# Two-block transformer on one core: the second head of each attention pair is normalised by GpSimd

## The chip, the cores and the metric

One core of a Trainium2 chip runs the whole program. The time is device microseconds of one launch, and the number to forecast is the median over several runs. In the texts "DVE" is VectorE, "ACT" ScalarE, "PE" TensorE, "POOL" GpSimd, "SP" SyncE.

## The reference

The input is x, 256 tokens by 1024 features, float32. A first block of two layers (feed-forward, mixer, cross attention to a memory, feed-forward) is followed by a second block of two layers (mixer of three parts, layer norm, feed-forward, layer norm). Three places hold the attention that the change touches:

```
# mixer of the first block's second layer (latent attention): 16 heads, 256 tokens, keys in the same or an earlier chunk of 64
sc = einsum('bhqd,bhkd->bhqk', q, k) * scale;  sc = where(chunk_mask, sc, -inf)
p = softmax(sc);  o = einsum('bhqk,bhkd->bhqd', p, v)
...
# second block, both layers (sparse attention): 8 heads of width 64
o_slc = selected attention, o_win = window attention      # both causal softmax attention at 256 tokens
o = gate[0] * o_cmp + gate[1] * o_slc + gate[2] * o_win
```

With 256 tokens every block of keys is selected and the window covers all, so the two sparse branches are 16 causal attention heads, each with its own gate.

## The kernel before

The kernel is written without a scheduler: each engine has its own program, and all of them walk the same list of pieces in the same order. The list of a stage comes from a hand-made string (WEAVE, one letter for each piece of a chain), so an engine's instructions stand in the order of the string, and semaphores alone connect the engines. A stage is named m0, m1 (mixers of the first block), c0, c1 (cross attention), f0 to f5 (feed-forward), b0, b1 (mixers of the second block). Weights come by DMA from SP into a ring of 6 buffers (ring), ACT rounds each buffer (w_hi) and DVE subtracts for the rest (w_lo), and PE multiplies with both.

The class Pairs (from L1184) is the attention of m1 and of b0 and b1. A piece ("A", (j, step)) treats pair j, that is two heads p = 0 and 1; there are 8 pairs in m1 and 8 in each of b0 and b1, 24 in all. Scores of a head lie in PSUM as 384 columns: 256 for the second half of the queries, 128 for the first half.

- Step 0: PE makes scores, DVE takes the row maxima (L175), ACT makes exponentials and their sums from PSUM into the head's SBUF buffer (L147).
- Step 1: DVE makes reciprocals of the four sums (L178), in b0 and b1 multiplies them by the gate (L158, 128x4), and scales each head's buffer in place: one TENSOR_SCALAR of 128x256 and one of 128x128 (L164). The second of the two signals "scaled" for its head. PE waits for "scaled" of head 0, transposes its three 128x128 blocks (L138), then does the same for head 1. ACT copies the transposed blocks out (L184, 128x384).
- Step 2: PE multiplies by the values, and the result is evicted.

In m1 the string puts step 1 of four pairs in a row, twice: once right behind the first scores, once near the stage's end, before the output product. In b0 and b1 the pairs are woven among the chains of the recurrent mixer (letters r and s), whose pieces also use POOL: piece "ru" masks three 128x1024 tiles (L158), and piece "nc" zeroes two small tiles (L197) and has DVE shift and add its input tiles (L185, L158 128x120) before PE's compression product.

POOL's part in m1 is only the squares for the next norm at the stage's end. In each stage POOL walks its pieces in the order of the string as well, and a wait holds up everything behind it on its queue.

```
# the step 1 of DVE, the lines that matter
        for p in range(2):
            x = A.s(j, p)
            e.ts(x[:, 0:256], x[:, 0:256], r[:, 2 * p + 1:2 * p + 2], None, MUL)
            e.ts(x[:, 256:384], x[:, 256:384], r[:, 2 * p:2 * p + 1], None, MUL).then_inc(*e.up("scaled", (A.name, j, p)))
```

Of the kernel before, what the change touches and what calls it, by code (L numbers as in the profile page):

```python
# [13 lines left out]
MUL, ADD, SUB, MIN, MAX = ALU.mult, ALU.add, ALU.subtract, ALU.min, ALU.max  # L14
# [665 lines left out]
def pool_x(e, K, s, j):  # L680

    n = AFTER[s]
    if j < 8 and n in NORMED:
        e.wait_ge(*K.x_at(s, j))
        x = K.x[:, j, :]
        if j == 0:
            e.then(e.tt(K.squares, x, x, MUL))
        else:
            e.then(e.tt(K.square, x, x, MUL), *(("squares", n) if j == 7 else ()))
            if j < 7:  # L690
                e.then(e.tt(K.squares, K.squares, K.square, ADD))
# [148 lines left out]
def pool_ln(e, K, s, what, i):  # L840
    half, dev, sq, M, squares = ln_area(K)
    x = K.x
    if what == "x" and 0 < i < 4:
        for k in (0, 1) if i == 1 else (i,):
            e.wait_ge(*K.at("evicted", (s, "x", last_of(s, k))))
        e.then(e.tt(half, x[:, 0, :] if i == 1 else half, x[:, i, :], ADD), *(("ln_half", s) if i == 3 else ()))
    elif what == "ld" and 0 < i < 7 and s[0] == "f":
        for k in (0, 1) if i == 1 else (i,):
            e.wait_ge(*centred(K, s, k))
            e.wait_ge(*K.at("ln_squares", (s, k)))  # L850
        e.tt(dev, x[:, 0, :] if i == 1 else dev, x[:, i, :], ADD)
        e.then(e.tt(sq, squares[:, 0, :] if i == 1 else sq, squares[:, i, :], ADD), *(("ln_added", s) if i == 6 else ()))
    elif what == "lm":
        e.wait_ge(*K.at("ln_means", s))
        for k in range(8):
            e.tt(x[:, k, :], x[:, k, :], M, SUB).then_inc(*e.up("ln_shifted", (s, k)))
# [327 lines left out]
class Pairs:  # L1184
# [20 lines left out]
    def stat(self, j, n, p=None):  # L1205
        c = self.stats[self.lane(j)][:, 4 * n:4 * n + 4]
        return c if p is None else c[:, 2 * p:2 * p + 2]

    def chains(self, what, names):
        out = {}  # L1210
        for name, js in zip(names, self.lanes):
            c = [(what, (js[0], 0)), (what, (js[0], 1))]
            for a, b in zip(js, js[1:]):
                c += [(what, (b, 0)), (what, (a, 2)), (what, (b, 1))]
            out[name] = c + [(what, (js[-1], 2))]
        return out
# [54 lines left out]
def dve_pairs(e, K, A, j, step):  # L1271
    if step == 0:
        for p in range(2):
            e.wait_ge(*K.at("scores", (A.name, j, p)))
            b, m = K.psum((A.name, j, "s", p)), A.stat(j, 0, p)
            e.red(m[:, 1:2], b[:, 0:256], MAX, negate=True)
            ins = e.red(m[:, 0:1], b[:, 256:384], MAX, negate=True)
            if not A.factor:
                ins.then_inc(*e.up("maxima", (A.name, j, p)))
        if A.factor:  # L1280
            e.then(ins)
            e.wait_ge(*K.at("factor", A.name))
            m = A.stat(j, 0).rearrange("p (a t) -> p a t", a=2)
            e.tt(m, m, A.factor(j), MUL).then_inc(*e.up("maxima", (A.name, j, None)))
    elif step == 1:
        for p in range(2):
            e.wait_ge(*K.at("evicted", (A.name, j, "s", p)))
        r = A.stat(j, 2)
        e.then(e.rec(r, A.stat(j, 1)))
        if A.gate:  # L1290
            r2 = r.rearrange("p (a q) -> p a q", a=2)
            e.then(e.tt(r2, r2, A.gate(j), MUL))
        for p in range(2):
            x = A.s(j, p)
            e.ts(x[:, 0:256], x[:, 0:256], r[:, 2 * p + 1:2 * p + 2], None, MUL)
            e.ts(x[:, 256:384], x[:, 256:384], r[:, 2 * p:2 * p + 1], None, MUL).then_inc(*e.up("scaled", (A.name, j, p)))


def in_lanes(what, units, lanes, steps=3):
# [10 lines left out]
def evenly(chains):  # L1310

    at = sorted(((n + 0.5) / len(c), k) for k, c in chains.items() for n in range(len(c)))
    return "".join(k for _, k in at)


def woven(stage, chains):

    for mark, piece in MARKS.items():
        chains[mark] = [(piece, i) for i in range(WEAVE.get(stage, "").count(mark))]
    its = {k: iter(c) for k, c in chains.items()}  # L1320
    return [next(its[k]) for k in WEAVE.get(stage) or evenly(chains)]
# [909 lines left out]


def pool_mla(e, K, T, what, i):
    if what == "x":
        pool_x(e, K, T.stage, i)

# [353 lines left out]

def pool_block(e, K, T, what, i):
    e.wait_ge(K.S.sem("loaded_c" + T.area), 16)
    s = T.stage
    if what in LN + ("x",):
        pool_ln(e, K, s, what, i)
    elif what[0] == "r":
        pool_delta(e, K, T, what, i)
    elif what[0] == "g":
        pool_gla(e, K, T, what, i)
    elif what == "nc" and i == 0:  # L2600
        e.wait_ge(*K.at("gated", (s, "g")))
        e.set(T.kc, 0.0)
        e.set(T.hid[0:64], 0.0).then_inc(*e.up("zeroed", (s, "hid")))
# [397 lines left out]
def pool_delta(e, K, T, what, i):  # L3001
    s, V = T.stage, T.block_of(what, i)
    m4 = T.c32.unsqueeze(2).broadcast_to([128, 4, 256])
    if what == "rp" and i == 0:
        e.wait_ge(*K.at("split_x", (s, 7)))
        e.set(T.PR[:, :, 0:1], 0.0).then_inc(*e.up("zeroed", (s, "PR")))
    elif what == "ri" and i == (0, 0):
        e.wait_ge(*K.at("turned", (s, "rtm", 3)))
        for n in [(s, "rp", 4), (s, "gp", 2), (s, "gl")] + [((s, "np", n), t) for n in range(3) for t in range(2)]:
            e.wait_ge(*K.at("summed", n))  # L3010
        e.set(T.Pt, 0.0)
        e.set(T.Q, 0.0)
        e.set(T.St[:, :, 0, :], 0.0).then_inc(*e.up("zeroed", (s, "r")))
    elif what == "ru" and i[1] == 1:
        tb = i[0]
        e.wait_ge(*K.at("evicted", (s, "rtm", 1)))
        e.wait_ge(*K.at("summed", (s, "ri", tb, (6, "r7"))))
        e.tt(V.Bm, bc(T.Btm[:, tb, :], 4), m4, MUL).then_inc(*e.up("masked", (s, tb, "B")))
        e.wait_ge(*K.at("evicted", (s, "rtm", 3)))
        e.tt(V.Vm, bc(T.Vtm[:, tb, :], 4), m4, MUL)  # L3020
        e.wait_ge(*K.at("evicted", (s, "ru", tb, 1)))
        e.tt(V.TUm, bc(V.AV, 4), m4, MUL).then_inc(*e.up("masked", (s, tb, "U")))
# [182 lines left out]
def pool_gla(e, K, T, what, i):  # L3205
    s = T.stage
    if what == "gd":
        for j in range(2):
            e.wait_ge(*K.at("evicted", (s, "gp", j)))
        e.tt(T.gE[2], T.gq, T.gk, MUL).then_inc(*e.up("pairs", s))  # L3210
    elif what == "gx" and i == 0:
        B = T.gB[:, :, 0:128]
        e.wait_ge(*K.at("scanned", (s, "g")))
        e.tt(T.XK[1][:, :, 0:128], B[:, :, 127:128].broadcast_to([128, 2, 128]), B, SUB).then_inc(*e.up("differences", (s, "x")))
    elif what == "ge" and i[1] == 0:
        n = i[0]
        h = HALVES[n]
        B, E = (a.rearrange("p k (c i) -> p k c i", i=2 * h) for a in (T.gB, T.gE[n % 3]))
        if n == 2:
            e.wait_ge(*K.at("summed", (s, "gd")))  # L3220
        elif n > 2:
            e.wait_ge(*K.at("scaled", (s, n - 3)))
        e.wait_ge(*K.at("scanned", (s, "g")))
        e.tt(E, B, B[:, :, :, h - 1:h].broadcast_to([128, 2, 128 // h, 2 * h]), SUB).then_inc(*e.up("differences", (s, n)))
# [219 lines left out]
ACTE = {"ffn": act_ffn, "mixer0": act_mixer0, "cross": act_cross, "mla": act_mla, "block": act_block}  # L3444
DVE = {"ffn": dve_ffn, "mixer0": dve_mixer0, "cross": dve_cross, "mla": dve_mla, "block": dve_block}
POOL = {"ffn": pool_ffn, "mixer0": pool_mixer0, "cross": pool_cross, "mla": pool_mla, "block": pool_block}

def stages(K):
# [149 lines left out]
```

## Time and profile before

| what | value |
|---|---|
| runs | 2096.41, 2089.3, 2094.63 us; median 2094.63 |
| profiled execution, its own time | 2091.17 us |
| its span | 2089.1 us |
| PE busy | 1971.4 us (94% of the span) |
| DVE busy | 1504.5 us (72%) |
| ACT busy | 1115.3 us (53%) |
| POOL busy | 400.7 us (19%), 357 instructions |
| chain that ended last | PE 82%, DVE 10%, ACT 5% |

The page gives busy time per engine over the whole span; which engine sets the pace differs from stage to stage, so the chain of waits and the timelines of the stages are read as well. The attention steps of m1 lie between about 855 and 887 us, those of b0 between 1300 and 1364 us, those of b1 between 1769 and 1851 us.

### The profile page before, as it was taken

How to read it: one execution, taken by the hardware profiler on the slowest of the kernel's cores; microseconds unless marked ns; L12 is line 12 of the kernel's file. 1: busy time of each engine (PE TensorE's matmuls, PEld its weight loads, DVE VectorE, ACT ScalarE, POOL GpSimd, SP SyncE). 2: the span in 40 equal slices, each digit the busy share in tenths (PEclk: the TensorE clock that was granted, in tenths of full speed). 3: DMA queues.
4: the chain of work that ended last, by engine and by line, in shares of the span. 5: the costliest groups of instructions: out<-in, count | busy, mean ns of one | idle time of the engine just before them, and what ended most of it. 6: DMA issues, size and time to landing. Idle time of an engine off the chain costs nothing.

```text
span 2089.1 us, 32759 instructions
## 1 busy us (share of the span) xinstructions
PE 1971.4 (94%) x12454; PEld 1720.6 (82%) x12454; DVE 1504.5 (72%) x2640; ACT 1115.3 (53%) x2048; POOL 400.7 (19%) x357
## 2 busy tenths in 40 slices
PE   7999999999999999899999997899998988899997
PEld 6888888888888887698888887688887877688886
DVE  6976876787678778768776696667756697567765
ACT  5654566565455556745554533556545444357554
POOL 3521002222112210023210101102213011101213
PEclk9999999999999999999999999999998999899999
DMA  7556443455565555135555321236553421225652
GB/s 252 197 175 194 159 131 122 132 190 178 186 191 188 174 190 165 55 121 194 187 179 176 125 88 41 87 111 219 189 176 110 139 76 41 77 94 169 191 182 82
DMA packets 88716, 309.81 MB, mean 148 GB/s; under 512 B 9840, under 2 KB 11632, under 8 KB 88176
## 3 DMA queue, kind: packets, MB, share of 16 engines
q1 hardware_dynamic: 88272, 305.03, 44.5%
q10 hardware_dynamic: 288, 2.69, 0.4%
q8 instruction: 99, 1.62, 0.3%
q14 instruction: 57, 0.47, 0.1%
HBM read 306.63 MB, written 1.05 MB: 147 GB/s over the span
## 4 chain that ended last, share of the span: by engine, by line
PE 82%; DVE 10%; ACT 5%; issue 2%; POOL 1%; DMA 1%; SPq 0%; DVEq 0%; ACTq 0%; POOLq 0%
PE ps L133 80%; DVE scratch L158 3%; ACT scratch L147 3%; PE ps L138 2%; POOL rows L158 1%; DVE w_lo L158 1%; DVE scratch L164 1%; DVE scratch L185 1%; DVE stats L175 1%; DVE x L158 1%; ACT w_hi L147 1%; DMA ring<-in_w 1%; DVE scratch L170 0%; ACT scratch L184 0%; ACT L152 0%
## 5 line engine op out<-in xcount | busy, mean ns | idle before, releaser
L133 PE MATMUL ps<-h,w_hi 128*128 128x512 f32 (+1 forms) x2912 | 903.0, 371 | 27.6 <-DVE w_lo L158 15.9
L158 DVE TENSOR_TENSOR w_lo<-ring,w_hi 128x1024 fp32r<-128x1024 f32 (+3 forms) x573 | 695.8, 1225 | 301.0 <-ACT w_hi L147 297.3
L147 ACT ACTIVATE w_hi<-ring 128x1024 fp32r<-128x1024 f32 (+3 forms) x573 | 583.5, 1029 | 419.1 <-PE ps L133 414.4
L133 PE MATMUL ps<-h,w_lo 128*128 128x256 f32 x2512 | 709.7, 283 | 0.0
L133 PEld LDWEIGHTS ps<-h,w_hi 128*128 128x128 f32 x2912 | 529.3, 192 | 132.0 <-issue 20.0
L133 PEld LDWEIGHTS ps<-h,w_lo 128*128 128x128 f32 x2512 | 481.2, 192 | 0.0
L133 PE MATMUL ps<-f,w_hi 128*128 128x512 f32 (+1 forms) x1444 | 419.1, 357 | 0.1
L133 PE MATMUL ps<-f,w_lo 128*128 128x256 f32 x1184 | 332.5, 281 | 0.0
L158 POOL TENSOR_TENSOR f<-f_work,f 128x256 fp32r<-128x256 f32 x132 | 188.0, 1425 | 583.3 <-ACT f L147 583.2
L133 PEld LDWEIGHTS ps<-f,w_hi 128*128 128x128 f32 x1444 | 254.9, 189 | 43.2 <-DVE scratch L158 0.3
L133 PEld LDWEIGHTS ps<-f,w_lo 128*128 128x128 f32 x1184 | 224.5, 190 | 0.1
L133 PE MATMUL ps<-scratch 64*128 64x128 f32 (+10 forms) x1696 | 196.4, 317 | 22.2 <-DVE scratch L158 10.2
L133 PEld LDWEIGHTS ps<-scratch 64*128 64x128 f32 (+4 forms) x1696 | 160.0, 180 | 54.0 <-issue 21.0
L184 ACT ACTIVATE scratch<-ps 128x512 f32<-128x512 f32 (+9 forms) x196 | 90.8, 487 | 195.6 <-PE ps L133 157.2
L158 POOL TENSOR_TENSOR rows<-x 128x256 f32<-128x256 f32 x64 | 54.1, 846 | 478.8 <-DVE x L158 470.0
L158 DVE TENSOR_TENSOR f_work<-f_work,ps 128x256 f32<-128x256 f32 x306 | 126.4, 414 | 3.6 <-ACT f_work L184 3.5
L158 DVE TENSOR_TENSOR f_work<-f_work 128x256 f32<-128x256 f32 x264 | 114.2, 433 | 8.6
L133 PE MATMUL ps<-w_hi,h 128*128 128x512 f32 (+2 forms) x384 | 113.9, 374 | 0.7 <-DVE w_lo L158 0.7
L184 ACT ACTIVATE f_work<-ps 128x256 f32<-128x256 f32 x306 | 110.9, 365 | 1.3 <-PE ps L133 1.3
L138 PE MATMUL ps<-consts,scratch 128*128 128x128 f32 (+3 forms) x428 | 68.5, 296 | 32.5 <-DVE scratch L164 12.9
L147 ACT ACTIVATE scratch<-ps,stats 128x256 f32<-128x256 f32 (+2 forms) x143 | 68.8, 500 | 48.0 <-PE ps L133 27.1
L158 DVE TENSOR_TENSOR scratch<-scratch 128x512 f32<-128x512 f32 (+7 forms) x108 | 69.5, 669 | 29.1 <-ACT scratch L184 24.4
(157 smaller groups left out, 2026.5 us busy)
## 6 DMA issues: line engine op xcount, KB each, us to landing
ring<-in_w SPq DMA_DIRECT2D x518, 512.0 KB, 4.0
ring<-in_w SPq DMA_DIRECT2D x48, 384.0 KB, 3.7
ring<-in_w SPq DMA_DIRECT2D x16, 396.0 KB, 3.1
ring<-in_w SPq DMA_DIRECT2D x8, 256.0 KB, 5.4
stage_consts<-in_ctwo ACTq DMA_DIRECT2D x1, 1346.0 KB, 6.0
stage_consts<-in_cthree ACTq DMA_DIRECT2D x1, 1283.0 KB, 6.4
x<-in_x SPq DMA_DIRECT2D x4, 256.0 KB, 6.7
scratch<-in_m SPq DMA_DIRECT2D x1, 1024.0 KB, 10.4
```

What stands on the lines that cost most here:

```text
L133: return self.e.matmul(out, lhsT, rhs, start=start, stop=stop, skip_group_check=free)
L138: return self.e.transpose(out, x, self.K.ident[0:x.shape[0], 0:x.shape[0]])
L147: return self.e.activation(out, x, func, **k)
L158: return self.e.tensor_tensor(out, a, b, op)
L164: return self.e.tensor_scalar(out, a, s1, None, op0)
L175: return self.e.tensor_reduce(out, a, AX, op, negate=negate)
L184: return self.e.activation(out, a, ACT.Copy)
L185: return self.e.tensor_copy(out, a)
```

## The change

DVE still makes the reciprocals and the gate product. It then copies the two reciprocals of head 1 into two spare columns of the statistics (share, columns 12 and 13 of the lane's 16), signals "shares", and scales head 0 alone. A new function on POOL waits for "shares" and scales head 1, as two TENSOR_TENSOR multiplications with the reciprocal broadcast along the row. The string of pieces is the same.

```
+    def share(self, j):
+        return self.stats[self.lane(j)][:, 12:14]
...
-        for p in range(2):
-            x = A.s(j, p)
-            e.ts(x[:, 0:256], x[:, 0:256], r[:, 2 * p + 1:2 * p + 2], None, MUL)
-            e.ts(x[:, 256:384], x[:, 256:384], r[:, 2 * p:2 * p + 1], None, MUL).then_inc(*e.up("scaled", (A.name, j, p)))
+        x = A.s(j, 0)
+        e.cp(A.share(j), r[:, 2:4]).then_inc(*e.up("shares", (A.name, j)))
+        e.ts(x[:, 0:256], x[:, 0:256], r[:, 1:2], None, MUL)
+        e.ts(x[:, 256:384], x[:, 256:384], r[:, 0:1], None, MUL).then_inc(*e.up("scaled", (A.name, j, 0)))
+
+
+def pool_pairs(e, K, A, j, step):
+    if step == 1:
+        x, r = A.s(j, 1), A.share(j)
+        e.wait_ge(*K.at("shares", (A.name, j)))
+        e.tt(x[:, 0:256], x[:, 0:256], r[:, 1:2].broadcast_to([128, 256]), MUL)
+        e.tt(x[:, 256:384], x[:, 256:384], r[:, 0:1].broadcast_to([128, 128]), MUL).then_inc(*e.up("scaled", (A.name, j, 1)))
...
 def pool_mla(e, K, T, what, i):
+    if what == "A":
+        pool_pairs(e, K, T.A, *i)
...
 def pool_block(e, K, T, what, i):
     e.wait_ge(K.S.sem("loaded_c" + T.area), 16)
+    if what == "A":
+        pool_pairs(e, K, T.A_, *i)
```

On DVE in m1, step 1 of one pair and the start of the next, before the change:

```order
L178 RECIPROCAL stats<-stats 128x4
L164 TENSOR_SCALAR scratch<-scratch,stats 128x256
L164 TENSOR_SCALAR scratch<-scratch,stats 128x128
L164 TENSOR_SCALAR scratch<-scratch,stats 128x256
L164 TENSOR_SCALAR scratch<-scratch,stats 128x128
L178 RECIPROCAL stats<-stats 128x4
```

and after it:

```order
L178 RECIPROCAL stats<-stats 128x4
L185 COPY stats<-stats 128x2
L164 TENSOR_SCALAR scratch<-scratch,stats 128x256
L164 TENSOR_SCALAR scratch<-scratch,stats 128x128
L178 RECIPROCAL stats<-stats 128x4
```

Two of the four scalings of a pair are gone from DVE and a copy of two columns has come in; in b0 and b1 the gate product stands between the reciprocal and the copy.

On POOL in b0, around the first pair's step 1 (the two groups of 128x1024 are the masks of the recurrent mixer's two halves, the memsets belong to piece "nc"):

```order
 L197 MEMSET scratch 128x2x128
 L158 TENSOR_TENSOR scratch<-scratch,stage_consts 128x1024 x3
+L158 TENSOR_TENSOR scratch<-scratch,stats 128x256
+L158 TENSOR_TENSOR scratch<-scratch,stats 128x128
 L197 MEMSET scratch 128x60
 L197 MEMSET scratch 64x256
 L158 TENSOR_TENSOR scratch<-scratch,stage_consts 128x1024 x3
```

The first pair's scaling now stands ahead of the memsets and of the second half's three masks; the other seven pairs of b0 stand behind those masks. In b1 four pairs stand ahead of the memsets and four behind the second half's masks.

## Rows read from the trace of the kernel before

**Rows 1.** The page: span and busy time of the engines.

```profile
span 2089.1 us, 32759 instructions
PE 1971.4 (94%) x12454; PEld 1720.6 (82%) x12454; DVE 1504.5 (72%) x2640; ACT 1115.3 (53%) x2048; POOL 400.7 (19%) x357
```

**Rows 2.** Groups by shape on DVE: busy us, mean ns of one, idle before.

```profile
L164 DVE TENSOR_SCALAR scratch<-scratch,stats 128x256 f32<-128x256 f32 x68 | 24.8, 375 | 1.3
L164 DVE TENSOR_SCALAR scratch<-scratch,stats 128x128 f32<-128x128 f32 x52 | 14.6, 280 | 0.0
```

**Rows 3.** Timeline of DVE in m1: start us, length us, instructions merged.

```profile
860.47 0.16 DVE L178 RECIPROCAL stats<-stats 128x4 f32<-128x4 f32 x1
860.67 1.01 DVE L164 TENSOR_SCALAR scratch<-scratch,stats 128x256 f32<-128x256 f32 x4
861.59 0.17 DVE L178 RECIPROCAL stats<-stats 128x4 f32<-128x4 f32 x1
...
864.06 1.01 DVE L164 TENSOR_SCALAR scratch<-scratch,stats 128x256 f32<-128x256 f32 x4
866.21 0.69 DVE L185 COPY scratch<-ps 96x512 f32<-96x512 f32 x1 [1.14 <-PE ps L138]
...
879.04 0.17 DVE L178 RECIPROCAL stats<-stats 128x4 f32<-128x4 f32 x1
...
883.55 1.22 DVE L158 TENSOR_TENSOR w_lo<-ring,w_hi 128x1024 fp32r<-128x1024 f32 x1
```

**Rows 4.** Chain that ended last, m1 and b0: start us, length us, what.

```profile
864.75 1.41 PE ps L138 x10
...
881.07 3.81 PE ps L138 x18
...
1344.13 0.98 PE ps L138 x6
...
1352.52 9.48 PE ps L133 x80
```

**Rows 5.** Groups by shape on POOL: busy us, mean ns, idle before.

```profile
L158 POOL TENSOR_TENSOR rows<-x 128x256 f32<-128x256 f32 x64 | 54.1, 846 | 478.8 <-DVE x L158 470.0 <-DMA consts<-in_cfix 3.5 <-DMA x<-in_x 2.6
```

**Rows 6.** Timeline of POOL: short and long cases of its shapes.

```profile
907.13 0.72 POOL L158 TENSOR_TENSOR rows<-x 128x256 f32<-128x256 f32 x1
907.93 0.81 POOL L158 TENSOR_TENSOR rows<-rows 128x256 f32<-128x256 f32 x1
...
1059.43 1.57 POOL L158 TENSOR_TENSOR f<-f_work,f 128x256 fp32r<-128x256 f32 x1 [4.08 <-ACT f L147]
...
1220.28 1.04 POOL L158 TENSOR_TENSOR scratch<-scratch 128x512 f32<-128x512 f32 x1 [2.12 <-DVE scratch L158]
...
1307.13 3.75 POOL L158 TENSOR_TENSOR scratch<-scratch,stage_consts 128x1024 f32<-128x1024 f32 x2 [15.92 <-PE ps L133]
```

**Rows 7.** Timeline of DVE in b0, from the first pair's step 1.

```profile
1308.26 0.18 DVE L178 RECIPROCAL stats<-stats 128x4 f32<-128x4 f32 x1
1308.47 0.57 DVE L158 TENSOR_TENSOR stats<-stats,scratch 128x4 f32<-128x4 f32 x1
1309.08 2.60 DVE L164 TENSOR_SCALAR scratch<-scratch,stats 128x256 f32<-128x256 f32 x4
1311.60 0.85 DVE L185 COPY scratch<-scratch 64x512 f32<-64x512 f32 x2
...
1314.55 1.13 DVE L158 TENSOR_TENSOR scratch<-scratch,stage_consts 128x120 f32<-128x120 f32 x4
...
1341.62 0.17 DVE L178 RECIPROCAL stats<-stats 128x4 f32<-128x4 f32 x1
```

**Rows 8.** Timeline of PE in b0 and b1: transposes behind step 1.

```profile
1361.82 1.57 PE L138 MATMUL ps<-consts,scratch 128*128 128x128 f32 x12
...
1776.11 2.94 PE L138 MATMUL ps<-consts,scratch 128*128 128x128 f32 x12 [2.87 <-DVE scratch L164]
...
1790.67 0.98 PE L138 MATMUL ps<-consts,scratch 128*128 128x128 f32 x6 [0.94 <-DVE scratch L164]
```

**Rows 9.** Stretches: us, busy (instructions) of PE, PEld, DVE, ACT, POOL, clock, DMA, GB/s.

```profile
879.04:884.88 5.84, 4.79 (x26) 4.29 (x28) 5.59 (x22) 3.25 (x7) 0.00 (x0) 0.71 0.00 0
```

## The prediction

> **What bounds the kernel now.** I first read the page [rows 1]: PE is busy 94% of the span, DVE 72%, POOL 19%. That makes POOL look free and DVE worth relieving, but it is an average, so the next view is the chain that ended last in the three stages with paired attention [rows 4]. There the chain does run through step 1. In m1 it goes through DVE's reciprocals and scalings from 860.47 us on, and only then to PE's transposes. The reader is to see two things there. In the first group of four pairs DVE takes 1.13 us a pair (reciprocal at 860.47, the next at 861.59), the last scalings start at 864.06, and PE's last ten small products follow at 864.75 until 866.17 [rows 3, 4]. So that group is bound by step 1: 5.7 us from first reciprocal to last product, and DVE's next work, the copy at 866.21, waits for PE, not the other way round. In the second group (first reciprocal 879.04) PE itself is the bound: 18 transposes in 3.81 us, until 884.88, that is 5.84 us after the reciprocal [rows 3, 4], at a mean granted clock of 0.71 of the full 2.4 GHz, so a part of it at 1.2 GHz; PE had been waiting before it rose [rows 9]. Nothing else is there for PE to do meanwhile: the queue is in order, and the output product stands behind the transposes.
>
> **What is removed.** A pair's four scalings show 375 and 280 ns each in the mean [rows 2], but they overlap: four take 0.92 us from start to start of the next instruction [rows 3], so two are worth 0.46 us. Over 24 pairs DVE loses 11 us of work. It gains 24 copies of two columns; no row has that shape, the nearest small one is the reciprocal of 128x4 at 0.16 us [rows 3]; overlapped I take 0.1, bounds 0 and 0.2. Net, DVE is relieved by about 8.6 us. On the path this is worth nothing by itself: PE takes the pair's heads in order and must have head 1 as well, and what follows on DVE waits for PE.
>
> **What is added.** POOL multiplies 128x256 and 128x128. With its neighbour idle it takes 1.04 us for 512 columns and 3.75 for twice 1024, 1.88 each [rows 6], so 0.84 us per 512 and 0.2 us that is fixed; that makes 0.62 and 0.41 for 256 and 128. The 256-column rows read 0.72 and 0.81 [rows 6]; I take 0.70 and 0.42, with 0.08 between instructions (907.13 + 0.72 to 907.93), in all 1.2 us a pair. The bounds are 1.0 and, since the mean of such a row is 0.85 [rows 5], 1.5. The VectorE half took 0.46. The Trainium skill (GPSIMD Engine Reference, section "4.1 Engine selection" and the measured table above it) puts elementwise work with two inputs on VectorE and gives 4497 ns for 2048 columns on GpSimd. That is 2.2 ns a column where the rows here give 1.64; by the page (an estimate) a pair would cost 0.2 us more and the sum below would be some 3 us higher. The rows are used.
>
> **The lock between the two engines.** The decisive rows are in b0. While POOL masks two tiles (1307.13, 3.75 us), DVE's four scalings take 2.60 us instead of 1.01, and end just after POOL does [rows 6, 7]. In m1, with POOL idle, the same four take 1.01 [rows 3]. It works the other way too: POOL's 128x256 takes 1.57 us when a w_lo split of DVE runs, against 0.72 to 0.81 [rows 6]. So a scaling on DVE and a multiplication on POOL exclude each other for whole instructions; the reciprocal at 1308.26 ran unhindered at 0.18 [rows 7]. The Trainium skill (SBUF — State Buffer, "SBUF: two separate sides") states it as an exclusive lock on a shared port pair: whichever of the two starts first holds it for its whole instruction. This trace agrees, with 2.60 us against 1.01. By a free sharing of the port the sum would be 2094 instead of 2105 (first rival).
>
> **m1, step by step.** From the reciprocal: copy done at 0.36, POOL could start at 0.41, but DVE's two scalings hold the port until about 0.8 or alternate with it. From then on each pair needs, one after the other, POOL's 1.12 and DVE's copy and two scalings, 0.5, so about 1.65 us a pair where it was 1.13. Head 1 of the fourth pair is ready at about 7.05 us instead of 4.55. Behind it PE has three transposes and the four other products, 1.0 with the signal, so the group ends at 8.2 instead of 5.7: **+2.5**. Second group: ready at 7.05, three transposes, end at 7.7 instead of 5.84: **+1.9**. The w_lo split at 883.55 moves with it but is still ahead of its product. Together +4.4. POOL has no other work here.
>
> **b0 and b1.** A lone pair has been 2.1 us from reciprocal to last transpose (gate product included). New: reciprocal, gate product, copy and two scalings to 1.0, POOL to 2.2, signal and three transposes to 2.8: +0.7. For two pairs in a row, 3.5 before (reciprocal at 1341.62, end of the transposes at 1345.11 [rows 4, 7]), the second head 1 is ready at 4.0, since the second gate product, copy and scalings alternate with POOL; the end is 4.6: +1.1.
> - b0: a lone pair that the chain passes through (its transposes end where PE's 80 products begin, 1352.52 [rows 4]) +0.7, another at 1331 +0.7, the two at 1341 +1.1, the last two, whose twelve transposes in 1.57 us feed ACT's copies [rows 8], +1.2.
> - b0's first pair: POOL's queue now has it ahead of three masks. Before, the masks cost DVE some 2.2 us while it was at the scalings. Now the pair goes first and the masks fall on the shifts and adds at 1311.60 to 1315.7 [rows 7], which feed PE's next product. DVE's port work of 4.1 us and POOL's 4.85 then follow each other, up to 2.6 us later than before; less the alternation I take +2.0. All b0: +5.7.
> - b1: the pairs at 1773 to 1779 (twelve transposes [rows 8]) +0.9, at 1789 to 1793 (six and six [rows 8]) +0.95, at 1823 +0.95, at 1843 +0.45, where other products lie between. All b1: +3.25.
>
> **Sum.** 4.4 + 5.7 + 3.25 = +13.4 us on the profiled execution's own 2091.17 us (span 2089.1 [rows 1] plus 2 around it): 2104.6. That execution is 3.5 us below the median of the three runs, and inside their spread, so I forecast **2105 us**, 0.5% slower. With the lower bounds (no lock in half the places, POOL 1.0) the sum is +5, with the upper ones (1.5 a pair, each on the path) +19.
>
> **Rivals.**
> 1. The engines hardly hinder each other on such short instructions. Then head 1 is late only by POOL's own length: m1 +1.0 and +0.3, a lone pair +0.3, two in a row +0.2, in all about +3: 2094 us. For it: POOL's instructions fit between DVE's; against it: the 2.60 us [rows 7].
> 2. DVE is what PE waits for, and relief of 8.6 us comes through as the time: 2082.5 us, faster. The mechanism is the end of a group of four in m1, where DVE's 1.13 us a pair would fall to about 0.75, and the same in b0 and b1. It decides when POOL's share of a pair takes less than DVE's old 0.46 us for it plus what PE needs for head 0. PE's three transposes take some 0.5, so POOL would have to be under 1.0 with no lock. Against it: 0.72 us for 128x256 alone [rows 6].
> 3. The delays grow: longer waits of PE bring longer stretches at the lower of the two clocks behind them, as the 0.71 after a wait shows [rows 9]; or POOL's in-order waits for "shares" hold up masks that the recurrent mixer needs, and the weights' loads start later in turn. I price this at the whole upper bound, +19 to +24: 2112 us.
> 4. The instruction stream could leave POOL's part hidden because PE has other work in front of it in b0 and b1: only m1's +4.4 is left, 2096 us.
>
> **Chances.** Forecast 0.64, rival 1 0.08, rival 2 0.05, rival 3 0.14, rival 4 0.09. A difference of 0.3%, 6.3 us, is about what measurements of this kernel can tell from none. The forecast's own spread puts some of its cases under 6.3 us. So: faster 0.05, same 0.18, slower 0.77. The range of 8 in 10 is 2096 to 2113: it takes in rival 4, half of rival 3 and both bounds of POOL's price, and leaves out rivals 1 and 2.
>
> **What would show it.** In m1 the reciprocals of a group should stand some 1.5 us apart instead of 1.13, DVE's scalings should show single cases of 0.7 us and more, and PE's waits before the transposes should be put down to POOL. POOL gains 48 instructions and 28 to 40 us of busy time; DVE loses 24 instructions net. From 860.47's counterpart to the last product 8.2 us; in the second group 7.7. In b0 the shifts and adds behind the first pair should be stretched by the masks. If POOL's two instructions take under 1.0 us together and DVE's scalings stay at 1.01 for four, the lock is wrong and rival 1 holds. If PE does not wait for POOL in b0 and b1, rival 4 does.

## The result and the profile after

The changed kernel takes 2100.49 us in the median of 15 runs (2095.8 to 2113.17); the kernel before, run 15 times beside it, 2095.8 us (2089.3 to 2102.44). The ratio is 1.0039 with a 95% interval of 1.0027 to 1.005: slower by 8.2 us (5.7 to 10.5). The two medians by themselves stand only 4.7 us apart and the two means 5.9, so the size is less sure than the direction. One execution of warm_before took 4597.3 us, and it is left out everywhere. The forecast was 2105 us with 2096 to 2113 around it, and slower. The sum behind it was built from steps, though, and several of those were wrong. The profiled execution of the change has a span of 2100.3 us and a time of its own of 2102.36.

The page after, against [rows 1]:

```profile
span 2100.3 us, 32783 instructions
PE 1977.3 (94%) x12454; PEld 1721.9 (82%) x12454; DVE 1505.9 (72%) x2616; ACT 1115.5 (53%) x2048; POOL 422.9 (20%) x405
```

POOL has 48 instructions and 22 us more, as it should. DVE has 24 instructions fewer and yet 1.4 us more busy time. The relief did not arrive. Groups by shape after, of POOL's and DVE's shares of step 1 (busy us, mean ns of one, idle before), against [rows 2]:

```profile
L158 POOL TENSOR_TENSOR scratch<-scratch,stats 128x256 f32<-128x256 f32 x24 | 15.4, 644 | 185.2 <-DVE stats L185 184.6
L158 POOL TENSOR_TENSOR scratch<-scratch,stats 128x128 f32<-128x128 f32 x24 | 9.5, 394 | 0.0
```

```profile
L164 DVE TENSOR_SCALAR scratch<-scratch,stats 128x128 f32<-128x128 f32 x28 | 16.4, 585 | 0.0
L164 DVE TENSOR_SCALAR scratch<-scratch,stats 128x256 f32<-128x256 f32 x44 | 14.6, 348 | 0.4
...
L185 DVE COPY stats<-stats 128x2 f32<-128x2 f32 x24 | 4.1, 171 | 0.8
```

The small scaling went from 280 to 585 ns. In m1's first four pairs it begins while POOL's 128x256 runs and ends 0.08 us after POOL's does, in all four; the wait is counted as its own busy time. POOL needs 0.64 + 0.39 = 1.04 us a pair.

**m1.** DVE's timeline after (start us, length us, instructions merged), against [rows 3]:

```profile
859.02 0.16 DVE L178 RECIPROCAL stats<-stats 128x4 f32<-128x4 f32 x1
859.22 0.17 DVE L185 COPY stats<-stats 128x2 f32<-128x2 f32 x1
859.29 0.93 DVE L164 TENSOR_SCALAR scratch<-scratch,stats 128x256 f32<-128x256 f32 x2
860.15 0.16 DVE L178 RECIPROCAL stats<-stats 128x4 f32<-128x4 f32 x1
...
862.65 0.90 DVE L164 TENSOR_SCALAR scratch<-scratch,stats 128x256 f32<-128x256 f32 x2
865.01 0.69 DVE L185 COPY scratch<-ps 96x512 f32<-96x512 f32 x1 [1.47 <-PE ps L138]
```

Two scalings now last as long as four did, 0.90 against 1.01, and the reciprocals stand 1.11 us apart, against 1.13. PE in the same stretch, first the kernel before and then the change:

```profile
861.37 0.52 PE L138 MATMUL ps<-consts,scratch 128*128 128x128 f32 x3 [0.56 <-DVE scratch L164]
```

```profile
860.37 0.87 PE L138 MATMUL ps<-consts,scratch 128*128 128x128 f32 x6 [1.01 <-DVE scratch L164]
861.48 0.84 PE L138 MATMUL ps<-consts,scratch 128*128 128x128 f32 x6 [0.24 <-DVE scratch L164]
...
863.69 1.28 PE L138 MATMUL ps<-consts,scratch 128*128 128x128 f32 x10 [0.26 <-ACT scratch L184]
```

and POOL:

```profile
859.53 4.29 POOL L158 TENSOR_TENSOR scratch<-scratch,stats 128x256 f32<-128x256 f32 x8 [88.95 <-DVE stats L185]
```

PE waits for DVE's head 0, which comes 1.35 us after its reciprocal instead of 0.90; POOL's head 1 is then ready at once. The delay is paid once for a group, not once for a pair. Where a step's 1.11 us come from can be read from the single instructions of the second pair: from the reciprocal (860.15) by way of the copy to POOL's start (860.60) 0.45, then POOL's 128x256 until 861.25, 0.65, and there the next reciprocal starts. POOL's 128x128 runs beside that reciprocal and its copy. From the first reciprocal to the copy behind the group it is 865.01 − 859.02 = 5.99 us, against 866.21 − 860.47 = 5.74 [rows 3]: +0.25 where +2.5 was forecast. The second group, first the kernel before and then the change:

```profile
886.14 0.42 DVE L158 TENSOR_TENSOR m_lo<-ps,m_hi 128x256 fp32r<-128x256 f32 x1 [1.37 <-ACT m_hi L184]
```

```profile
877.85 0.17 DVE L178 RECIPROCAL stats<-stats 128x4 f32<-128x4 f32 x1
...
884.98 0.42 DVE L158 TENSOR_TENSOR m_lo<-ps,m_hi 128x256 fp32r<-128x256 f32 x1 [1.27 <-ACT m_hi L184]
```

It takes 7.13 us from its first reciprocal to the first m_lo residual, against 7.10, at a mean granted clock of 0.76 in both: nothing where +1.9 was forecast.

**A lone pair in b0**, in the chain that ended last, first the kernel before and then the change:

```profile
1350.43 0.19 DVE stats L178
```

```profile
1360.05 0.19 DVE stats L178
...
1360.63 0.82 DVE scratch L164 x2
...
1361.59 0.84 PE ps L138 x6
1362.43 0.86 PE ps L133 x5
```

From reciprocal to the end of the transposes 2.38 us, where the pair ending at 1352.52 [rows 4] had 2.09: +0.29, forecast +0.7.

**The first pair of b0**, DVE and then POOL, against [rows 6, 7]:

```profile
1311.04 0.18 DVE L178 RECIPROCAL stats<-stats 128x4 f32<-128x4 f32 x1
...
1311.53 0.90 DVE L164 TENSOR_SCALAR scratch<-scratch,stats 128x256 f32<-128x256 f32 x2
1312.35 2.99 DVE L185 COPY scratch<-scratch 64x512 f32<-64x512 f32 x2
1315.37 2.65 DVE L158 TENSOR_TENSOR scratch<-scratch,stage_consts 128x120 f32<-128x120 f32 x4
...
1318.94 1.13 DVE L158 TENSOR_TENSOR scratch<-scratch,stage_consts 128x120 f32<-128x120 f32 x4
```

```profile
1311.70 1.00 POOL L158 TENSOR_TENSOR scratch<-scratch,stats 128x256 f32<-128x256 f32 x2 [19.09 <-DVE stats L185]
...
1312.99 4.09 POOL L158 TENSOR_TENSOR scratch<-scratch,stage_consts 128x1024 f32<-128x1024 f32 x2
```

POOL's masks have slid behind its share of the pair and now hold up DVE's shifts and adds: two copies take 2.99 us instead of 0.85, the first four adds 2.65 instead of 1.15. From the reciprocal to the end of the last add it is 9.03 us, where it was 7.42 [rows 7]: +1.6, forecast +2.0. In the chain that ended last PE's next products start right behind the last add.

**b1.** Between the same two w_lo splits on either side of it b1 takes 112.0 us, and took 111.4: +0.7 where +3.25 was forecast. In b_only, whose b1 is the changed one too, it is 110.5. Over the whole trace no transpose of step 1 (L138) has a wait of PE put down to POOL.

### The profile page after: what moved, and what is told of

It is laid out like the page before. It is cut to its first block, busy times and chain, and to the rows that moved or that the text cites. A ratio compares the mean times of both kernels' runs of the same rounds, so it can differ in the third digit from the quotient of the medians.

```text
span 2100.3 us, 32783 instructions
## 1 busy us (share of the span) xinstructions
PE 1977.3 (94%) x12454; PEld 1721.9 (82%) x12454; DVE 1505.9 (72%) x2616; ACT 1115.5 (53%) x2048; POOL 422.9 (20%) x405
## 4 chain that ended last, share of the span: by engine, by line
PE 82%; DVE 10%; ACT 5%; issue 2%; POOL 1%; DMA 1%; SPq 0%; DVEq 0%; ACTq 0%; POOLq 0%
PE ps L133 80%; DVE scratch L158 3%; ACT scratch L147 3%; PE ps L138 2%; DVE w_lo L158 1%; POOL rows L158 1%; DVE scratch L185 1%; DVE scratch L164 1%; DVE stats L175 1%; DVE x L158 1%; ACT w_hi L147 1%; DMA ring<-in_w 1%; ACT scratch L184 0%; DVE scratch L170 0%; ACT L152 0%
## 5 line engine op out<-in xcount | busy, mean ns | idle before, releaser
L138 PE MATMUL ps<-consts,scratch 128*128 128x128 f32 (+3 forms) x428 | 68.8, 300 | 36.4 <-DVE scratch L164 15.2
L138 PEld LDWEIGHTS ps<-consts,scratch 128*128 128x128 f32 (+3 forms) x428 | 52.9, 151 | 48.8 <-issue 12.4
```

Of the source, the lines that this page charges most:

```text
L138: return self.e.transpose(out, x, self.K.ident[0:x.shape[0], 0:x.shape[0]])
```

## The experiments

Each was timed in five rounds against the kernel before on the same chip; ratios have 95% intervals. Three questions stood: do the engines really lock each other, which place costs what, and what does TensorE's clock add?

### Which stage

m1_only and b_only switch the change off in the other stages; b0_first_dve switches it off for b0's first pair alone. Where it is off, DVE scales both heads as before and POOL does nothing.

```diff
+def on_pool(A, j):
+    return A.name == "m1"                             # m1_only
+    return A.name != "m1"                             # b_only
+    return (A.name, j) != (("b0", "n"), 0)            # b0_first_dve
```

> Head 1 goes to POOL in the latent attention (m1, eight pairs) alone; b0 and b1 are as before. Theory L (the lock and POOL's length delay every pair, as forecast): m1 costs 4.4 us, so ratio 1.0021. Theory Q (the cost is in b0: the first pair's scaling has moved the masks on POOL's queue onto the shifts that feed PE, and PE's clock falls behind it): under 1 us here, ratio within 1.0005 of 1. Theory C (mostly TensorE's clock, wherever the waits of PE grow): also under 1 us, since PE's waits in m1 hardly grew in the trace of the changed kernel. In the trace: 1.1 us a pair in a group of four, both before and here.

> Head 1 goes to POOL in b0 and b1 alone, m1 as before. Theory L: 9 us of the 13.4, ratio 1.0043. Theories Q and C: the whole of the measured change, ratio 1.0035 to 1.004, nearly all of it between 1265 and 1365 us.

> The changed kernel, but the first pair of b0 keeps both heads on DVE, so POOL's masks stand where they stood. Theory Q: the shifts and adds of piece nc end as early as before, 1.6 us are won back there and some 1.5 us more of PE's products that now ran at 1.2 GHz: ratio 1.002 to 1.0025 instead of 1.0039. Theory L: one pair of 24 is undone, 0.7 us at most: ratio 1.0036. Theory C: as Q if the low clock at the products of nc goes with the delay, but the stretch at the two pairs around 1350 us stays.

m1_only: 2095.16 us against 2092.44, ratio 1.0009 (0.9992 to 1.0026). b_only: 2102.8, ratio 1.0047 (1.0029 to 1.0065). (All three theories expected some 1.004 of b_only.) So the change loses time without m1, and the rival that only m1 costs anything is out. That m1 takes next to none rests on the trace (+0.25 us above); m1_only's interval reaches 1.0026 and by itself doesn't exclude the forecast's 1.0021. b0_first_dve brings the place back to 7.44 us, with the old pattern in DVE's timeline:

```profile
1310.95 2.60 DVE L164 TENSOR_SCALAR scratch<-scratch,stats 128x256 f32<-128x256 f32 x4
1313.47 0.85 DVE L185 COPY scratch<-scratch 64x512 f32<-64x512 f32 x2
```

but its time is 2103.29, ratio 1.0049 (1.003 to 1.0068), not lower than b_only's, where 1.002 to 1.0025 was expected. Its executions had a mean granted clock of 0.974, b_only's of 0.977. That a place gives back 1.6 us and the whole doesn't is a miss; what the clock could have to do with it stands under "The clock".

### Order of POOL's queue alone

queue_only is the kernel before, with one wait added: POOL goes on to the masks of b0's second half only when DVE has the first pair's gate product. POOL scales nothing.

```diff
-            e.then(e.tt(r2, r2, A.gate(j), MUL))
+            e.then(e.tt(r2, r2, A.gate(j), MUL), "shares", (A.name, j))
...
+    if (s, what, i) == ("b0", "A", (0, 1)):
+        e.wait_ge(*K.at("shares", ((s, "n"), 0)))
```

> The kernel before, with one edit: POOL waits for the first pair's gate product in b0 before it masks, as the changed kernel makes it do, without scaling anything. Theory Q: DVE's shifts and adds behind the pair meet the masks and end 1 to 1.6 us later after the reciprocal than before; that is all: 1 to 3 us, ratio 1.001. If instead the masks cost the same wherever they fall (they blocked the four scalings before), no change: the time from reciprocal to the last add stays at 7.4 us.

DVE and POOL there:

```profile
1303.13 4.50 DVE L164 TENSOR_SCALAR scratch<-scratch,stats 128x256 f32<-128x256 f32 x4
1307.55 0.85 DVE L185 COPY scratch<-scratch 64x512 f32<-64x512 f32 x2
...
1310.50 1.13 DVE L158 TENSOR_TENSOR scratch<-scratch,stage_consts 128x120 f32<-128x120 f32 x4
```

```profile
1303.51 3.77 POOL L158 TENSOR_TENSOR scratch<-scratch,stage_consts 128x1024 f32<-128x1024 f32 x2
```

Four such scalings take 1.01, 2.60 or 4.50 us by when POOL's masks start. The place takes 8.92 us (reciprocal at 1302.72 to last add), 1.5 more than before, though POOL scales nothing: in the change 1.6 were lost there. Here the masks hold up the scalings and not the shifts and adds, so the sum is alike and the instructions that pay are others. The whole is at 2096.69 against 2091.04, ratio 1.0032 (1.0012 to 1.0053), where 1.001 was expected: some 5 us more than the place explains.

### Lock, and length of POOL's work

on_act gives POOL's share to ACT. pool_twice has POOL do both multiplications of head 1 twice, so that head is scaled twice and its part of the attention output differs. nocopy leaves DVE's copy out; POOL reads the reciprocals (in b0 and b1 the gate products) where they are.

```diff
 on_act, in act_pairs, step 1:
+        e.wait_ge(*K.at("shares", (A.name, j)))
+        e.act(x[:, 0:256], x[:, 0:256], ACT.Copy, scale=r[:, 1:2])
+        e.act(x[:, 256:384], x[:, 256:384], ACT.Copy, scale=r[:, 0:1]).then_inc(*e.up("scaled", (A.name, j, 1)))
 pool_twice, in pool_pairs, ahead of the two that are there:
+        e.tt(x[:, 0:256], x[:, 0:256], r[:, 1:2].broadcast_to([128, 256]), MUL)
+        e.then(e.tt(x[:, 256:384], x[:, 256:384], r[:, 0:1].broadcast_to([128, 128]), MUL))
 nocopy:
-        e.cp(A.share(j), r[:, 2:4]).then_inc(*e.up("shares", (A.name, j)))
```

> Head 1 is scaled by ACT instead of POOL (two activations from SBUF to SBUF with the same copied reciprocals). Nothing of it shares a port with DVE. Theory L (the exclusion between POOL and DVE costs the time): DVE's two scalings of head 0 take 0.46 to 0.5 us again instead of 0.90, and PE's first transposes come 0.4 us earlier for each pair; against it stands ACT's in-order queue, 0.8 us a pair. Ratio 1.001 to 1.003, under the changed kernel. If the time goes to the copy and the signal instead, the transposes start as late as in the changed kernel.

on_act's DVE in m1:

```profile
860.17 0.16 DVE L178 RECIPROCAL stats<-stats 128x4 f32<-128x4 f32 x1
...
860.44 0.54 DVE L164 TENSOR_SCALAR scratch<-scratch,stats 128x256 f32<-128x256 f32 x2
860.90 0.17 DVE L178 RECIPROCAL stats<-stats 128x4 f32<-128x4 f32 x1
```

With POOL silent the same two scalings take 0.54 us instead of 0.90, and reciprocals stand 0.73 apart: this is the relief that the second rival counted on, and POOL's part takes all of it. The time is worse, 2122.95, ratio 1.0159 (1.0131 to 1.0186), where 1.001 to 1.003 was expected: now PE waits for head 1 behind ACT's own work. PE in m1:

```profile
863.55 1.51 PE L138 MATMUL ps<-consts,scratch 128*128 128x128 f32 x6 [1.90 <-ACT scratch L147]
```

> The changed kernel with POOL's two multiplications done twice (head 1 is scaled twice, so its part of the result is another). POOL then needs 2.1 us a pair. If POOL's length is on the path, PE's step of a pair in m1 goes from 1.11 to about 2.2 us, m1 alone costs 8 us and the whole 15 to 20 us: ratio 1.012. If the recurrence were set by DVE and PE alone, with POOL hidden, the ratio stays near 1.005.

pool_twice: 2132.57, ratio 1.0196 (1.0167 to 1.0224), where 1.012 was expected, and PE's waits change hands:

```profile
866.32 0.85 PE L138 MATMUL ps<-consts,scratch 128*128 128x128 f32 x6 [0.86 <-POOL scratch L158]
868.34 0.91 PE L138 MATMUL ps<-consts,scratch 128*128 128x128 f32 x6 [1.18 <-POOL scratch L158]
```

A pair now takes 2.02 us. So POOL's 1.04 us fits, just, under the step of 1.11; another microsecond of it goes almost whole to PE. Twenty-four pairs at 0.9 are some 22 us, and the change alone costs 8; the other 10 or so of the 41 us are not shown. The mean granted clock was 0.966 there.

> The changed kernel without the copy of two reciprocals on DVE: POOL reads them where DVE wrote them and waits for the reciprocal or the gate product itself. A copy with its wait takes 0.17 us in the trace, and DVE's next scaling overlaps it. Theory L: POOL starts 0.2 us earlier and one turn at the port less for each of 24 pairs: up to 3 us less than the changed kernel, ratio 1.0025. Theories Q and C: the masks are as late as before the edit, 0.5 to 1 us less than the changed kernel, ratio 1.0035.

No theory had this one: 2106.09, ratio 1.006 (1.004 to 1.008), where 1.0025 to 1.0035 was expected. It lies above the change's 1.0039, though the intervals overlap. DVE, POOL and PE in m1's second group:

```profile
880.73 1.15 DVE L164 TENSOR_SCALAR scratch<-scratch,stats 128x256 f32<-128x256 f32 x2
```

```profile
882.04 1.02 POOL L158 TENSOR_TENSOR scratch<-scratch,stats 128x256 f32<-128x256 f32 x2 [0.25 <-DVE stats L178]
```

```profile
883.29 0.85 PE L138 MATMUL ps<-consts,scratch 128*128 128x128 f32 x6 [0.42 <-DVE scratch L164]
```

Without the copy, POOL starts right behind the reciprocal, at 880.78, only 0.04 us after DVE's first scaling. POOL's 128x256 runs through in 0.61 us, DVE's takes 0.80, and its two scalings together need 1.15 us instead of 0.90. Head 0, which PE needs first, is ready 1.49 us after the reciprocal instead of 1.35, and the pairs stand 1.27 apart. In this group the copy costs 0.17 us and earns more: with it DVE's 128x256 starts some 0.2 us ahead of POOL's and is done in 0.35. (In m1's first group of nocopy DVE starts 0.11 us ahead, the scalings take 0.91 and the pairs 1.03. So a few hundredths decide which engine goes through; what exactly decides is not shown.) Whether this makes the whole slower than the change isn't shown either: nocopy ran at a mean granted clock of 0.974.

### The clock

before_again is the kernel before, unchanged. warm_before and warm_after add four throwaway products for PE ahead of its wait for "scaled" of each pair in b0 and b1.

```diff
+        if p == 0 and A.name != "m1":
+            for n in range(4): pe_warm(e, K)
```

> The kernel before, unedited, as one more kernel: a control for every number here. The first profile of it had 6.8 us at the lower clock in b0, the changed kernel and the m1 variant 20.5, though b0 of the m1 variant is the old code. Theory C (the clock of b0 falls because of the change): this run has some 7 us at the lower clock in b0 and 101 us between the two weight splits that enclose it. Theory N (b0 falls into the longer stretches in any version, and the first profile was a lucky one): 14 to 21 us at the lower clock, 104 to 106 us. Ratio 1.000 within 0.0015 for both.

> The kernel before, with four 128x128 products into an idle bank ahead of PE's wait for head 0 of each pair of b0 and b1 (16 pairs). They fill 0.45 us of a wait that is 0.9 to 1.4 us where PE waits, and cost 0.45 us each where it does not (four or five pairs). Theory C (a part of the change's 8 us is PE running at the lower clock behind waits): less time at the lower clock in b0 and b1 than the 40 us between 1261 and 1846 us of the control, ratio 0.998 to 1.001. If the clock does not answer to it: ratio 1.001, by the products that are not hidden.

> The same four products in the changed kernel. Theory C: the changed kernel's surplus over the kernel before shrinks to what the steps themselves cost, some 4 us, so this run is slower than the other one with these products by 0.002 instead of 0.004, and the time at the lower clock is the same in both. If the clock has no part in it, the distance stays at 0.004.

before_again: 2093.5 against 2091.04, ratio 1.0008 (0.9985 to 1.0031); that is what no change looks like. The stretch of b0, 1261 to 1366 us, in four kernels: before, before_again, m1_only (whose b0 is the old code) and the change (columns as in [rows 9]):

```profile
1261.00:1366.00 105.00, 86.29 (x684) 69.06 (x682) 69.99 (x185) 47.27 (x136) 14.01 (x11) 0.97 0.15 54
```

```profile
1261.00:1366.00 105.00, 85.97 (x678) 69.27 (x676) 68.58 (x183) 45.99 (x133) 14.15 (x11) 0.97 0.15 53
```

```profile
1261.00:1366.00 105.00, 86.93 (x652) 68.01 (x651) 67.44 (x181) 45.40 (x132) 14.16 (x11) 0.90 0.13 45
```

```profile
1261.00:1366.00 105.00, 83.78 (x621) 68.00 (x620) 63.95 (x156) 43.05 (x124) 20.48 (x23) 0.90 0.15 54
```

The granted clock is 0.90 of 2.4 GHz in the change, so part of the stretch ran at 1.2 GHz. But m1_only has 0.90 there too, with the old code. The w_lo splits on either side of b0 give its length in each kernel, with the granted clock from 1261 to 1366 us:

| kernel | b0, us | clock |
|---|---|---|
| before | 101.3 | 0.97 |
| before_again | 102.6 | 0.97 |
| warm_before | 102.1 | 0.97 |
| masks_late | 99.2 | 0.97 |
| masks_late2 | 98.4 | 0.98 |
| m1_only (b0 as before) | 106.6 | 0.90 |
| queue_only | 104.8 | 0.93 |
| b0_first_dve | 105.6 | 0.93 |
| warm_after | 106.3 | 0.93 |
| b_only | 107.2 | 0.92 |
| nocopy | 109.3 | 0.90 |
| change | 109.3 | 0.90 |

The change is 8.0 us longer than the kernel before, 6.7 than its second execution, and 2.7 than m1_only, which ran at the same clock. So 2.7 is what the profiles show at a like clock, and the rest goes with the lower clock. Whose doing that is stays open: all six kernels with something delayed in b0 have 0.90 to 0.93, but so has one of the four with the old code there, and each is a single execution. (on_act and pool_twice reach b0 13 us and more later, and the stretch doesn't fit them.)

Over many executions the clock can be weighed. In the 77 executions of the kernel before that were timed beside the experiments, the mean granted clock lay between 0.973 and 0.982, and the time fell by 1.64 us for each 0.001 of it. Their mean is 2092.4 us at 0.9783; that of the change 2101.7 ± 1.2 at 0.9760. By that the clock's part of these 9.3 us is 2.3 × 1.64 = 3.8, and 5.5 are left. This is rough. The kernel before that ran beside the change itself averaged 2095.8 us, which makes it 5.9 us instead of 9.3, and its clocks are not on record; and a lower clock may be a result of longer waits as well as a cause of time. Weighed in the same way against their own partners, b_only has 5.6 of 9.3 us left, queue_only 5.2 of 7.2 and b0_first_dve 1.5 of 9.6, each uncertain by about 2. So at a like clock undoing b0's first pair may well have given something back.

The warm pair doesn't settle it. warm_before is slower than the kernel before by a ratio of 1.0018 (1.0 to 1.0036), where a part of the clock would have made it 0.998 to 1.001, and its b0 has the clock it had without the products. The two versions ran at the same mean clock (0.9779 and 0.9777), and their means, 2098.5 and 2101.2 us, stand 2.7 us apart (warm_after's ratio is 1.0029, 1.0013 to 1.0045). That is less than the change costs without the products, as the clock's part would have it, but the intervals overlap.

### A version that beats both

If DVE's time in b0 hangs on when POOL's masks run, the masks can be moved the other way. masks_late is the kernel before, and in b0 and b1 POOL waits with the second half's masks until DVE's shifts and adds of piece nc are done; after them PE works for some 9 us without DVE. masks_late2 has the first half's masks wait as well, for the copies of "k2".

```diff
 masks_late, pool_delta, piece ru:
+        if tb == 1: e.wait_ge(*K.at("shifted", (s, 1)))
 masks_late2:
+        e.wait_ge(*(K.at("shifted", (s, 1)) if tb else K.at("copied", (s, "k2", 0))))
```

> The kernel before, all scaling on DVE; POOL makes the second half's masks in b0 and b1 only when DVE has done the shifts and adds of piece nc (their product needs PE 10 us later). Theory Q says the masks cost what they block on DVE: in b0 the gate product and four scalings took 2.0 us more than elsewhere, in b1 the first copies 2.3 us. Both go: the reciprocal of b0's first pair to the last add takes 5.5 us instead of 7.4. 4 us less, ratio 0.998. If the masks are then late for PE's product, the gain comes back as a wait there.

> As the run with late masks, and the first half's masks wait too, until DVE has copied the third set of keys. In the trace of the kernel before, DVE's three multiplications of 128x256 take 3.78 us beside these masks and 0.82 without, in both b0 and b1, on the chain of waits. Theory Q: 3 us more in each stage, 10 us in all, ratio 0.995. Against it: the third mask and PE's masked products come later, and 2 us of it may come back in each stage: ratio 0.997.

masks_late in b0, DVE and POOL:

```profile
1304.15 1.01 DVE L164 TENSOR_SCALAR scratch<-scratch,stats 128x256 f32<-128x256 f32 x4
1305.07 0.85 DVE L185 COPY scratch<-scratch 64x512 f32<-64x512 f32 x2
```

```profile
1309.33 3.74 POOL L158 TENSOR_TENSOR scratch<-scratch,stage_consts 128x1024 f32<-128x1024 f32 x2 [22.64 <-DVE scratch L158]
```

The scalings are back at 1.01 us, the copies at 0.85, and the place takes 5.45 us instead of 7.42. The masks run while DVE waits for PE. Between its splits b0 takes 99.2 us instead of 101.3, and b1 108.4 instead of 111.4. The time is 2090.24 against 2094.17, ratio 0.9976 (0.9956 to 0.9997), where 0.998 was expected: small, at the limit of what five rounds tell, and the only version whose whole interval lies below 1. masks_late2 has the same 5.45 us, but its first half's masks now fall on other copies. DVE and POOL:

```profile
1284.91 3.70 DVE L185 COPY scratch<-scratch 128x256 f32<-128x256 f32 x2
```

```profile
1282.49 5.64 POOL L158 TENSOR_TENSOR scratch<-scratch,stage_consts 128x1024 f32<-128x1024 f32 x3 [14.59 <-DVE scratch L185]
```

These two took 2.13 us in masks_late. Against that, the three multiplications of 128x256 that the first half's masks used to hold up take 0.82 us instead of 3.78. Ratio 0.9987 (0.997 to 1.0005), where 0.995 to 0.997 was expected: nothing gained over masks_late.

## Why the prediction was right, and where not

- **Direction: right, for the reason given.** POOL and DVE exclude each other on these instructions. Shown by on_act (0.54 against 0.90 us), by queue_only (1.01, 2.60, 4.50 for four such scalings) and by DVE's busy time, which rose. The Trainium skill's exclusive lock (SBUF — State Buffer, "SBUF: two separate sides") holds here, with 585 ns against 280 for the small scaling. Its price of 2.2 ns a column on GpSimd (GPSIMD Engine Reference, the table above "4.1 Engine selection"), by which the forecast's pair would have been 1.4 us (the prediction's estimate), fits less well here: 1.04 was measured. The rival of free sharing is out by its mechanism, and so is the one in which the relief comes through: the reciprocals went from 1.13 to 1.11 apart, not to 0.75. The size of the steps, though, is nearer to the first rival's +3 than to the forecast's +13.4.
- **Wrong: "From then on each pair needs, one after the other, POOL's 1.12 and DVE's copy and two scalings, 0.5, so about 1.65 us a pair".** Measured 1.11. POOL takes 1.04, so my price for it was near (its 22 us of busy time lie below the 28 to 40 forecast, and it was 48 instructions as said). But the second term hardly adds. By the starts and lengths of the instructions, DVE's first scaling has mostly run before POOL's first gets going, the second ends just behind POOL's first, and reciprocal and copy go on beside POOL's second. So a step is 0.45 us until POOL starts and 0.65 of POOL's 128x256. I added lengths where I should have laid them out in time. m1's +4.4 is +0.3; lone pairs are +0.3 instead of +0.7, for the same reason. b1's +3.25, made up of such pairs, is +0.7. PE's waits are put down to DVE, not to POOL; by my last test that would have meant the fourth rival, and b_only's 1.0047 shows that the test was wrong. My test of "single cases of 0.7 us and more" was the right place to look: the small scaling takes up to 0.67.
- **Right: b0's first pair.** POOL's queue order put the masks on the shifts and adds; +2.0 forecast, +1.6 measured, and queue_only shows that the masks' moment alone costs as much (1.5), without any work of POOL's on the pair.
- **Missing from the sum: the clock.** It stood as a rival only. The steps as measured give m1 +0.3, b0 +2.7 at a like clock and b1 +0.7, some 4 us in all, where 13.4 were forecast. The rest of the measured difference, 1 to 4 us, goes with a mean clock of 0.976 instead of 0.978. Whether the change's longer waits cause the lower clock stays open.
- **The number was near by luck.** The sum was three times too large, and 13.4 lies above the interval of 5.7 to 10.5. What brought it back is that it was added to 2091.17 us, the profiled execution's time, and the kernel before came out at 2095.8, and that the clock's part was left out. From 2095.8 the same sum would have given 2109.

## What to carry to other kernels

- Work moved from VectorE to GpSimd frees VectorE only if what VectorE does meanwhile isn't held up by GpSimd's instructions. Measure the neighbour's instruction lengths, not its instruction count: here 280 ns became 585 and the busy time rose.
- Ask first when GpSimd's long instructions run. One wait ahead of two masks cost 0.32% (0.12 to 0.53), nearly as much as the whole change with its 24 heads (0.39%), though only 1.5 us of it are seen at the place; and one that moved them the other way was the only gain. Put them where VectorE waits for TensorE.
- In a kernel whose granted clock varies, take a profile of the unchanged kernel a second time before laying microseconds of one stretch to a change: the same b0 code took 101.3, 102.6 and, in m1_only, 106.6 us.

## What the runs showed that was not expected

- Leaving out a copy of 0.17 us made each pair of m1's second group 0.16 us longer (1.27 against 1.11): POOL's multiplication then went through ahead of DVE's scaling. In the first group the pairs got shorter (1.03).
- DVE's reciprocal of 128x4 is not held up by POOL (0.17 us in every kernel). The small gate product of 128x4 is at times: for b0's first pair 0.57 us [rows 7] and 0.17 after, and once in b1 1.87 us in both kernels.
- The same kernel varies with its mean granted clock: executions of the kernel before at 0.981 to 0.982 average 2086.6 us, those at 0.975 to 0.976 about 2097. At a like clock, 0.978, it still averaged 2089.9 us on one chip and 2094.0 on another.
